# Paged key products: a GpSimd addition of the two halves of each head ahead of VectorE's sum

## The reference

```python
k_past = cache_sb_k[l][page_table].reshape(DB, past, SB_HEADS, SB_DIM)      # 8, 4096, 8, 64
z = jnp.einsum('bqhd,bshd->bhqs', qi, kf) * Dh ** -0.5 + bias               # q . k of every past key
l1mb = jnp.where(mask, jax.nn.log_sigmoid(-z), 0.0)
after = lax.cumsum(l1mb, axis=3, reverse=True) - l1mb
A = jnp.where(mask, jnp.exp(jax.nn.log_sigmoid(z) + after), 0.0)
return jnp.einsum('bhqs,bshd->bqhd', A, vf)
```

## Time and profile before

| | us |
|---|---|
| median of 3 runs | 1597.4 (1591.54 to 1603.41) |
| profiled execution | 1599.24 |
| its span, first to last instruction | 1597.2 |
| TensorE busy | 1295.1 |
| VectorE busy | 844.9 |
| ScalarE busy | 484.7 |
| GpSimd busy | 359.5 |

### The profile page before, as it was taken

How to read it: one execution, slowest core, us unless ns; L and a number is a source line. 1 busy time by engine, 2 the same in 40 slices (tenths; PEclk the granted TensorE clock), 3 DMA queues, 4 the chain that set the end, 5 groups by cost and what they waited for, 6 DMA issues and landing times. The chain is left out here.

```text
span 1597.2 us, 23116 instructions
## 1 busy us (share of the span) xinstructions
PE 1295.1 (81%) x7719; PEld 1084.3 (68%) x7719; DVE 844.9 (53%) x1198; ACT 484.7 (30%) x902; POOL 359.5 (23%) x235
## 2 busy tenths in 40 slices
PE   3549588897798953887969889499999999597997
PEld 3449466766676553787958779387878787265885
DVE  4425787887986612837757468344444443323221
ACT  5312434444446521142231421331313130312110
POOL 0027634343340000625425245100000000000000
PEclk9969798898999977998989899799999899798998
DMA  3536667376373504554345543186555542543320
GB/s 132 158 117 210 214 186 239 100 231 192 126 238 106 169 30 138 164 180 132 119 140 159 180 132 108 49 241 191 162 184 168 179 146 90 172 133 130 105 74 32
DMA packets 200420, 237.89 MB, mean 149 GB/s; under 512 B 13539, under 2 KB 122434, under 8 KB 200298
## 3 DMA queue, kind: packets, MB, share of 16 engines
q1 hardware_dynamic: 196338, 224.61, 45.3%
q0 software_dynamic: 3968, 11.87, 2.1%
HBM read 215.88 MB, written 20.64 MB: 148 GB/s over the span
## 5 line engine op out<-in xcount | busy, mean ns | idle before, releaser
L248 PE MATMUL bank<-xh,b_w_hi 128*128 128x344 f32 x480 | 166.1, 346 | 56.9 <-ACT b_mix L257 17.5
L1961 POOL TENSOR_TENSOR cp_keys<-cp_keys,cp_q 128x1024 f32<-128x1024 f32 x64 | 163.1, 2568 | 158.7 <-DMA cp_keys<-cache_sb_k 158.4
L1961 POOL TENSOR_TENSOR bp_keys<-bp_keys,bp_q 128x1024 f32<-128x1024 f32 x64 | 156.8, 2472 | 180.0 <-DMA bp_keys<-cache_sb_k 172.0
L248 PE MATMUL bank<-xl,b_w_hi 128*128 128x344 f32 x480 | 161.4, 336 | 0.0
L248 PE MATMUL bank<-xh,b_w_lo 128*128 128x344 f32 x480 | 161.1, 336 | 0.0
L248 PE MATMUL bank<-xh,d_w_hi 128*128 128x344 f32 x384 | 131.3, 342 | 24.4 <-DVE d_w_lo L231 16.7
L317 PE MATMUL bank<-xh,c_w_hi 128*128 128x344 f32 x384 | 130.1, 339 | 17.3 <-DVE c_w_lo L303 17.3
L248 PEld LDWEIGHTS bank<-xh,b_w_hi 128*128 128x128 f32 x480 | 97.6, 203 | 61.5 <-ACT b_w_hi L226 27.3
L317 PE MATMUL bank<-xl,c_w_hi 128*128 128x344 f32 x384 | 126.5, 330 | 0.0
L317 PE MATMUL bank<-xh,c_w_lo 128*128 128x344 f32 x384 | 126.4, 329 | 0.0
L248 PE MATMUL bank<-xl,d_w_hi 128*128 128x344 f32 x384 | 126.2, 329 | 0.0
(11 more groups left out here) (381 smaller groups left out, 2609.0 us busy)
## 6 DMA issues: line engine op xcount, KB each, us to landing
cp_keys<-cache_sb_k SPq DMA_DIRECT2D x128, 256.0 KB, 2.9
cp_values<-cache_sb_v SPq DMA_DIRECT2D x128, 256.0 KB, 2.8
bp_keys<-cache_sb_k SPq DMA_DIRECT2D x128, 256.0 KB, 3.1
dp_values<-cache_sb_v SPq DMA_DIRECT2D x128, 256.0 KB, 2.8
b_w_raw<-w_in SPq DMA_DIRECT2D x20, 512.0 KB, 4.0
c_w_raw<-w_in SPq DMA_DIRECT2D x16, 512.0 KB, 5.0
d_w_raw<-w_in SPq DMA_DIRECT2D x16, 512.0 KB, 5.2
o_mix<-mix SPq DMA_DIRECT2D x8, 1024.0 KB, 5.9
```

Of the source, the lines that this page charges most:

```text
L248: last = self.nc.tensor.matmul(self.bank(j, c)[:, 0:self.width], w[:, s, k, :], x[:, k, c * self.width:(c + 1) * self.width], start=(k == ...
L1961: self.nc.gpsimd.tensor_tensor(self.keys[:, s], self.keys[:, s], q, ALU.mult).then_inc(self.scaled.sem, 1)
```

## The change

The multiplication no longer tells VectorE that a pair is ready. It adds to a new semaphore `multiplied`; GpSimd waits for it, then adds the second 32 products of every head to the first 32, in place, and this addition adds to `scaled`. VectorE sums the first 32 numbers of each head. The order of all other instructions is as before.

```diff
-        self.scaled, self.z_ready, self.biased = S("scaled", NP), S("z_ready", NP), S("biased", 1)
+        self.multiplied, self.scaled, self.z_ready, self.biased = S("multiplied", NP), S("scaled", NP), S("z_ready", NP), S("biased", 1)
...
     def setup_pool(self, pool):
+        self.multiplied.credit(pool)
         self.scaled.credit(pool)
...
         q = self.q[:].rearrange("p (o c) -> p o c", o=1).to_broadcast([P, 2, GW])
-        self.nc.gpsimd.tensor_tensor(self.keys[:, s], self.keys[:, s], q, ALU.mult).then_inc(self.scaled.sem, 1)
+        self.nc.gpsimd.tensor_tensor(self.keys[:, s], self.keys[:, s], q, ALU.mult).then_inc(self.multiplied.sem, 1)
+        pool.wait_ge(self.multiplied.sem, self.multiplied.at(i, r + 1))
+        halves = self.keys[:, s].rearrange("p r (h f d) -> p r h f d", h=SBH, f=2)
+        self.nc.gpsimd.tensor_tensor(halves[:, :, :, 0, :], halves[:, :, :, 0, :], halves[:, :, :, 1, :],
+                                     ALU.add).then_inc(self.scaled.sem, 1)
...
         self.nc.vector.tensor_reduce(self.z[:, i % 2, :, 2 * r:2 * r + 2].rearrange("p h r -> p r h"),
-                                     self.keys[:, r % self.ring].rearrange("p r (h d) -> p r h d", d=SBD), AXX,
+                                     self.keys[:, r % self.ring].rearrange("p r (h f d) -> p r h f d", h=SBH, f=2)[:, :, :, 0, :], AXX,
                                      ALU.add).then_inc(self.z_ready.sem, 1)
```

## The result

The changed kernel takes 1652.8 us (median of 4 runs, 1651.1 to 1658.7) against 1596.9 for the kernel before beside it: a ratio of 1.0355, 95% interval 1.0308 to 1.0401, +56 us. The forecast was 1626 with a range of 1604 to 1650, so the direction was right and the size was half of the truth, just outside the range. The profiled execution took 1653.3 (span 1651.3), 54 more than the 1599.2 of before.

A forecast was written before the change was run, and what follows sets the result against it. In the prompt attention and mLSTM, TensorE and VectorE are busiest; cost arises where they wait for GpSimd's products. 10.6 + 8.5 + 4.5 + 4.5 + 0 = +28 on 1599.2 gives 1627.3, against the median 1626; range 1604 to 1650.

The forecast's parts named there:

- Place (a): Ahead of the first attention piece: sample 0's twelve chained pairs end later, +10.6 us, in front of TensorE's 13.18 us stall.
- Place (b): mLSTM's first head: seven pairs back to back delay the turned keys' copy (L1639), +8.5 us; heads 1 to 3 booked none.
- Place (c): Last pairs of an mLSTM head, ahead of the denominators (L1693): +2.0 us in heads 1 and 2, +0.5 and 0 elsewhere, +4.5 together.
- The price of a pair: GpSimd time per key pair: product 2.36, wait 0.07, addition 1.23, so 3.66 us instead of 2.36; VectorE's sum 0.684.
- the other estimate, 1.11: Addition of 512 pairs of numbers priced from the Trainium skill's 2.6 cycles per element at 1.2 GHz: 1.11 us.
- This wait covers it: mLSTM heads 1 to 3: L1639's wait for ScalarE, 4.0 us at most, hides the later products; otherwise up to 3.9 a head.
- The shared port: GpSimd work keeps some VectorE instructions from starting: scans 0, L1647 +1.5 in each of heads 1 to 3, +4.5 us.
- with -7 and +10 as ends: Prompt attention loops: VectorE's 8.5 us a head saved against longer port waits, booked 0, between -7 and +10 us.
- the port goes the other way: Rival: each addition holds back one VectorE instruction as a product does, 3 x 5 for scans, +5 in loops: 1646, chance 0.14.
- VectorE's saving: 128 reductions read half as much, 0.53 us less each, 68 us of VectorE in all; attention loops booked at 0.
- TensorE waited for VectorE only 21.6 and 10.9 us: Attention loops: TensorE's waits for VectorE at its two main places in four heads, the first mostly for softplus; loops booked 0.

The follow-up runs named there:

- e14: Kernel before, no additions, with VectorE itself making key products 1, 3, 5, 8, 11 and 14 of each mLSTM head: 1574.4 us (0.9868).
- e18: Kernel before with eight small GpSimd memsets behind each product, VectorE still summing all 64 products a head: 1604.0 us (1.0047).

## Why the forecast was half right

**What bounds, and where the waits are: right.** Places (a), (b) and (c) all show; nothing outside the two stages moved.

**The price of a pair: right.** Addition 1.25 (1.23; the other estimate, 1.11, was too low), sum 0.68 (0.684), the wait 0.08 (0.07). The whole GpSimd time, 549 us, is over the 525 of the terms because additions are held in turn.

**Place (a): right in size, +9.4 us in the stall (10.6).** The second piece came 12 us later.

**Place (b): right for the first head (11.1 against 10.6), wrong for the others.** "This wait covers it; without it the price would be up to 3.9 us a head" was a failing step, though not the costliest: the cover was 4.0 us at most, and the waits became 14 us in three heads, 4.7 each. The step compared the cover with the additions alone. In fact the seven sums also started later, by 3.7 us in head 1, because the instructions behind the scans (L2018, L1627, L1630) are held too, now that the first four pairs take 15.0 us and not 9.4.

**Place (c): about right in size.** TensorE's wait at L1810 grew by 3.3 us (7.7 to 11.0), and 4.5 were booked.

**The terms of time as a sum: not measured cleanly.** 10.6 + 8.5 + 4.5 = 24 us were booked for products that are ready later. The run with this time, long sums and small memsets gave +7, but its openings gave something back. The bare delay for place (a) cost its full length.

**The shared port: this is the term that failed, by its size.** The mechanism was named and each instance well priced (L1647 in head 1: 10.1 us from 6.9, and +3.1 was forecast ahead of what the sums give back; at a join more than one scan got through, as forecast, and eight took 7.4 us from 9.7). But it was booked for two lines, at +4.5, and set at 0 for the loops, "with -7 and +10 as ends". From memsets to additions the step is +78 with long sums and +66 with short, and by the estimate above at least 61 and 46 of that belong to the hold; 33 and 25 us of the step lie in the attention stage, which was booked at 0. The forecast's rival, "the port goes the other way", came nearest, with 1646 and a chance of 0.14, and it too was priced by three places and not by all.

**VectorE's saving: not 0.** The sums are worth 14 us without additions and 30 with them. "TensorE waited for VectorE only 21.6 and 10.9 us" was read as: VectorE doesn't set the pace. It does in part, and the more so the more it is held. The forecast has only about 7 us of the saving in it, 0.5 at the end of each chain and 4.8 at L1647. The two errors, the hold too small by 56 to 74 us and the saving by 23, cancel in part, and time may have been booked too high. That the forecast came as near as 27 us is partly luck.

**The clock: not in the sum.** 10 us of the mLSTM's 35 are the same matmuls at a mean granted clock of 0.88 instead of 0.91. The stage in which TensorE stood least (e14, 0.93) had the fewest, 324 us. Whether the waits alone lower it is not shown: e18 has 84 us of idle time at 0.89, the kernel after 102 at 0.88.

## What to carry to other kernels

Before work is added to GpSimd, list every VectorE instruction that is held by GpSimd in the trace, and count how much of VectorE's time falls beside the new work. Three places in sight are not enough: here the held time grew by 73 us in 78 more instructions. Each addition took 1.25 us of GpSimd to spare VectorE 0.53, and through the hold VectorE lost a little more than it was spared (850.3 us busy against 844.9). To price the time without the hold, run the time without the work, but look at VectorE's busy time in that run: if it is under that of the kernel before, as here, the stand-in also opens gaps, and its result is not the price of time alone.

## What the runs showed of the hardware

- A GpSimd addition of 128x512, a product of 128x1024 and a copy of 128x512 keep VectorE's two-input instructions out until they end, and wait for these in turn. A memset of 128x512 doesn't keep them out: scans took 0.19 us and L1630 0.34 beside it, as alone. L1647's copies, one tensor in, are kept out by the memset too (0.59 us, alone 0.27).
- Additions exchanged for two memsets each made the mLSTM 42 us shorter (446 to 404).
- VectorE's sums (TENSOR_REDUCE, 0.68 and 1.21 us) took the same time beside any GpSimd work, 0.69 and 1.23 at most.
- Where one product followed another directly, one held scan of 32 columns passed at each join. With GpSimd's wait for itself between (0.08 us), three passed behind a product, and one where an addition was followed directly by the next product. A 512-column scan stood through four products, 10.5 us, where none of them waited for itself; with a small memset behind each product the longest took 3.6.
- A GpSimd copy of 128x512 took 0.61 us alone and up to 1.57 where it waited for VectorE; each small memset with its wait for itself 0.156 us.
